# Attention weights times values as three split products, in a hybrid encoder layer on one core

## The reference

```python
def diff_attention(q, k, v, lam, lambda_init, subln_g, rel_table):
    ...
        logits = jnp.einsum('bqhcd,bkhcd->bhcqk', qblk, k,
                            preferred_element_type=F32) * scale + bias[None, :, None]
        p = jax.nn.softmax(logits, axis=-1)
        attn = p[:, :, 0] - lam * p[:, :, 1]
        return jnp.einsum('bhqk,bkhe->bqhe', attn.astype(v.dtype), v)
    ...
    out = rmsnorm(out, subln_g) * (1.0 - lambda_init)
```

## Time and profile before

| | |
|---|---|
| median of 3 runs | 969.24 us (969.03 to 969.33) |
| profiled execution | 969.0 us, its span 967.2 us |
| TensorE busy | 960.2 us, 5755 matmuls |
| VectorE busy | 664.1 us |
| ScalarE busy | 440.0 us |
| GpSimd busy | 88.1 us |

### The profile page before, as it was taken

The page is one execution under the profiler, slowest core; times in us unless marked ns, Lnnn a source line. Parts: engine busy times, 40 slices in busy tenths (PEclk is TensorE's granted clock), DMA queues, the critical chain, the costliest instruction groups (busy, mean ns, idle before and its releaser), DMA issues.

```text
span 967.2 us, 15550 instructions
## 1 busy us (share of the span) xinstructions
PE 960.2 (99%) x5755; PEld 839.7 (87%) x5755; DVE 664.1 (69%) x999; ACT 440.0 (45%) x699; POOL 88.1 (9%) x104
## 2 busy tenths in 40 slices
PE   9999999999999999999999999999999999999998
PEld 7889999999888887677777878889999999988887
DVE  6887886777754438868898755788787677743333
ACT  6445665546333233234454563446565554622222
POOL 0011121210011010000000000011111121000100
PEclk9999999999999999999999999999999999999999
DMA  7356777674433346121221332246777767333322
GB/s 233 136 144 171 197 175 192 167 192 139 138 98 100 98 127 238 66 86 48 82 85 44 124 106 91 99 137 159 188 187 182 190 171 183 99 104 99 89 70 87
DMA packets 55031, 128.69 MB, mean 133 GB/s; under 512 B 5955, under 2 KB 14288, under 8 KB 54725
## 3 DMA queue, kind: packets, MB, share of 16 engines
q1 hardware_dynamic: 44452, 107.31, 34.2%
q0 software_dynamic: 10384, 20.67, 12.3%
q10 hardware_dynamic: 144, 0.05, 0.1%
HBM read 123.78 MB, written 4.22 MB: 132 GB/s over the span
## 4 chain that ended last, share of the span: by engine, by line
PE 94%; DVE 3%; issue 1%; ACT 1%; DMA 0%; DVEq 0%; SPq 0%; ACTq 0%
PE bank L2151 14%; PE bank L2153 14%; PE bank L2152 14%; PE bank L2198 12%; PE bank L2199 12%; PE bank L2200 12%; PE bank L2639 1%; PE bank L2640 1%; PE bank L2641 1%; PE bank L2531 1%; PE bank L2285 1%; PE bank L2286 1%; PE bank L2287 1%; ACT prob L960 0%; PE bank L2365 0%
## 5 line engine op out<-in xcount | busy, mean ns | idle before, releaser
L1216 DVE TENSOR_TENSOR w_lo<-raw,w_hi 128x1024 fp32r<-128x1024 f32 (+1 forms) x94 | 113.3, 1205 | 110.2 <-ACT w_hi L630 109.9
L630 ACT CAST w_hi<-raw 128x1024 fp32r<-128x1024 f32 (+1 forms) x94 | 95.0, 1011 | 187.5 <-PE bank L2153 172.4
L2198 PE MATMUL bank<-xt_hi,w_hi 128*128 128x256 f32 x544 | 154.2, 284 | 0.0
L2199 PE MATMUL bank<-xt_lo,w_hi 128*128 128x256 f32 x544 | 153.9, 283 | 0.0
L2200 PE MATMUL bank<-xt_hi,w_lo 128*128 128x256 f32 x544 | 153.9, 283 | 0.0
L2151 PE MATMUL bank<-x_hi,w_hi 128*128 128x512 f32 x320 | 128.5, 402 | 0.1
L2152 PE MATMUL bank<-h_lo,w_hi 128*128 128x512 f32 x330 | 128.4, 389 | 0.0
L2153 PE MATMUL bank<-x_hi,w_lo 128*128 128x512 f32 x320 | 124.8, 390 | 0.0
L2152 PE MATMUL bank<-x_lo,w_hi 128*128 128x512 f32 x320 | 124.7, 390 | 0.0
L2199 PE MATMUL bank<-xt_lo,wt_hi 128*128 128x256 f32 x408 | 115.5, 283 | 0.0
L2200 PE MATMUL bank<-xt_hi,wt_lo 128*128 128x256 f32 x408 | 115.5, 283 | 0.0
(11 more groups left out here) (370 smaller groups left out, 1856.5 us busy)
## 6 DMA issues: line engine op xcount, KB each, us to landing
raw<-in_ffn_w_down SPq DMA_DIRECT2D x32, 512.0 KB, 3.5
raw<-in_ffn_w_gate SPq DMA_DIRECT2D x25, 512.0 KB, 4.4
raw<-in_ffn_w_up SPq DMA_DIRECT2D x25, 512.0 KB, 4.5
raw<-in_w_in SPq DMA_DIRECT2D x24, 512.0 KB, 3.3
raw<-in_ffn_w_gate SPq DMA_DIRECT2D x34, 256.0 KB, 3.2
raw<-in_ffn_w_up SPq DMA_DIRECT2D x34, 256.0 KB, 3.1
raw<-in_ffn_w_down SPq DMA_DIRECT2D x16, 384.0 KB, 3.1
sums<-in_ffn_w_gate SPq DMA_DIRECT2D x17, 256.0 KB, 3.9
```

The source lines that it names most:

```text
L630: nc.scalar.copy(w_hi[:, half, 0:kb, :], raw[:, slot, 0:kb, :]).then_inc(w_hi_made, 1)
L1216: nc.vector.tensor_tensor(w_lo[:, half, 0:kb, :], raw[:, slot, 0:kb, :], w_hi[:, half, 0:kb, :].bitcast(F32), ALU.subtract).then_inc(w_spl ...
L2198: nc.tensor.matmul(dst, high[:, k, :], xt_hi[ffn][:, m, k, :], start=start and k == 0, stop=False, skip_group_check=True)
L2199: nc.tensor.matmul(dst, high[:, k, :], xt_lo[ffn][:, m, k, :], start=False, stop=False, skip_group_check=True)
```

## The change

The product of weights and values is made as three split products. ScalarE's copies of the turned weights and values now cast to fp32r (`attn_hi`, `v_hi`), and VectorE makes the low parts (`attn_low`, `v_low`), each as the difference of the bank and the high part. The low parts lie where the folded values of the Hyena part (`vx`) and the bias were, for head 3 also in a part of `x0c`. A turn now waits until VectorE has read its bank too (`attn_split` in place of `attn_t_set`). ScalarE's cast of projection weights for one tile per head moves behind the last copies. Two semaphores are taken out and two added (`v_split`, `attn_split`): the landing of the lambdas is counted with another load, and one wait in the filters is made with the chain semaphore of VectorE.

```diff
-        v_nat, _ = place("v_nat", [P, NT, P], at=act3_at)
+        v_hi, _ = place("v_hi", [P, NT, P], F32R, at=act3_at)
+        v_lows = [place(f"v_lo{n}", [P, NT, P], F32R, at=at)[0] for n, at in enumerate((vx_at + 4 * S, bias_at))]
+        attn_hi, _ = place("attn_hi", [P, NT, S], F32R, at=attn_t_at)
+        attn_lows = [place(f"attn_lo{n}", [P, S], F32R, at=at)[0]
+                     for n, at in enumerate((vx_at + 4 * 2 * S, vx_at + 4 * 3 * S, x0c_at + 4 * 3 * S))]
+
+        def v_low_part(h):
+            return v_lows[h == 3]
+
+        def attn_low_part(h, kt):
+            return attn_lows[1 if kt % 2 else 2 * (h == 3)]
...
-                act.wait_ge(mlp_landed, 16)
+                act.wait_ge(mlp_landed, 32)
...
-                nc.scalar.copy(v_nat[:], bank[TURN_BANKS[h]][:].rearrange("p (t c) -> p t c", t=NT)).then_inc(v_set, 1)
+                nc.scalar.copy(v_hi[:], bank[TURN_BANKS[h]][:].rearrange("p (t c) -> p t c", t=NT)).then_inc(v_set, 1)
...
-                    nc.scalar.copy(attn_t[:, kt, :], bank[4 + kt % 2][:]).then_inc(attn_t_set, 1)
+                    nc.scalar.copy(attn_hi[:, kt, :], bank[4 + kt % 2][:]).then_inc(attn_t_set, 1)
...
             attn_turns(0, (0, 1))
-            split(8, N_MIX + 15)
             qk_high(1, 1)
             attn_turns(0, (2, 3))
+            split(8, N_MIX + 15)
             attended(0)
...
-                    nc.vector.tensor_tensor(hsum[:, 0, :], total, decay[:, 0, :], ALU.mult).then_inc(filt_read, 1)
-                    dve.wait_ge(filt_read, 1)
+                    link(nc.vector.tensor_tensor(hsum[:, 0, :], total, decay[:, 0, :], ALU.mult))
...
+            def v_low(h):
+                dve.wait_ge(v_set, h + 1)
+                nc.vector.tensor_tensor(v_low_part(h)[:], bank[TURN_BANKS[h]][:].rearrange("p (t c) -> p t c", t=NT),
+                                        v_hi[:].bitcast(F32), ALU.subtract).then_inc(v_split, 1)
+
+            def attn_low(h, kt):
+
+                dve.wait_ge(attn_turned, NT * h + kt + 1)
+                dve.wait_ge(attn_t_set, NT * h + kt + 1)
+                nc.vector.tensor_tensor(attn_low_part(h, kt)[:], bank[4 + kt % 2][:], attn_hi[:, kt, :].bitcast(F32),
+                                        ALU.subtract).then_inc(attn_split, 1)
...
             combine(0, 3)
+            v_low(0)
             cross_far(0)
             split(8, N_MIX + 14)
+            attn_low(0, 0)
             project(13)
             split_qk(1, 0)
+            attn_low(0, 1)
+            attn_low(0, 2)
             split_qk(1, 1)
+            attn_low(0, 3)
             own_near(0)
             split(8, N_MIX + 15)
...
             hy_low(3)
+            v_low(3)
+            attn_low(3, 0)
+            attn_low(3, 1)
             split(8, N_OUT + 1)
+            attn_low(3, 2)
+            attn_low(3, 3)
             split(8, N_OUT + 2)
...
             def turn(h, kt):
-                wait(pe, attn_t_set, NT * h + kt - 1)
+                wait(pe, attn_split, NT * h + kt - 1)
...
-                pe.wait_ge(v_set, h + 1)
+                pe.wait_ge(v_split, h + 1)
                 for kt in range(NT):
                     pe.wait_ge(attn_t_set, NT * h + kt + 1)
-                    ins = nc.tensor.matmul(bank[6][:], v_nat[:, kt, :], attn_t[:, kt, :], start=kt == 0, stop=kt == NT - 1)
+                    nc.tensor.matmul(bank[6][:], v_hi[:, kt, :], attn_hi[:, kt, :], start=kt == 0, stop=False)
+                    nc.tensor.matmul(bank[6][:], v_low_part(h)[:, kt, :], attn_hi[:, kt, :], start=False, stop=False)
+                    pe.wait_ge(attn_split, NT * h + kt + 1)
+                    ins = nc.tensor.matmul(bank[6][:], v_hi[:, kt, :], attn_low_part(h, kt)[:], start=False, stop=kt == NT - 1)
                     if kt + 2 < NT:
                         turn(h, kt + 2)
```

More of the change, by code:

```diff
@@ L281, in build @@
         x_landed = [sem(f"x_landed{k}") for k in range(KD)]
-        ident_landed, cols_landed, mlp_landed, lam_landed, dft_landed, late_landed, filt_landed = (
-            sem(n) for n in ("ident_landed", "cols_landed", "mlp_landed", "lam_landed",
+        ident_landed, cols_landed, mlp_landed, dft_landed, late_landed, filt_landed = (
+            sem(n) for n in ("ident_landed", "cols_landed", "mlp_landed",
                              "dft_landed", "late_landed", "filt_landed"))
@@ L309, in build @@
             sem(n) for n in ("proj_read", "score_sum", "logit_set", "prob_set", "attn_set", "r0_set"))
-        v_turned, v_set, attn_turned, attn_t_set, pv_sum, att_sq, att_o_set = (
-            sem(n) for n in ("v_turned", "v_set", "attn_turned", "attn_t_set", "pv_sum", "att_sq", "att_o_set"))
+        v_turned, v_set, v_split, attn_turned, attn_t_set, attn_split, pv_sum, att_sq, att_o_set = (
+            sem(n) for n in ("v_turned", "v_set", "v_split", "attn_turned", "attn_t_set", "attn_split", "pv_sum", "att_sq", "att_o_set"))
         tap_set, vx_set, vx_turned, vx_nat_set = (
@@ L423, in others @@
                 sp.dma_start(z_t[:], a["c_z"]).then_inc(mlp_landed, 16)
-                sp.dma_start(lam_in[:].rearrange("p k d -> p (k d)"), a["lambdas"].to_broadcast([P, 4 * DK])).then_inc(lam_landed, 16)
+                sp.dma_start(lam_in[:].rearrange("p k d -> p (k d)"), a["lambdas"].to_broadcast([P, 4 * DK])).then_inc(mlp_landed, 16)
                 sp.dma_start(rel[:], a["rel_bias"]).then_inc(late_landed, 16)
@@ L1096, in _ @@
             attn_turns(1, (0, 1))
-            split(8, N_MIX + 19)
             qk_high(2, 1)
             attn_turns(1, (2, 3))
+            split(8, N_MIX + 19)
             attended(1)
@@ L1112, in _ @@
             attn_turns(2, (0, 1))
-            split(8, N_MIX + 23)
             qk_high(3, 1)
             attn_turns(2, (2, 3))
+            split(8, N_MIX + 23)
             attended(2)
@@ L2004, in _ @@
             imaginary_parities(0)
+            v_low(1)
             project(16)
@@ L2007, in _ @@
             cross_near(1)
+            attn_low(1, 0)
             project(17)
             split_qk(2, 0)
+            attn_low(1, 1)
+            attn_low(1, 2)
             split_qk(2, 1)
+            attn_low(1, 3)
             cross_far(1)
@@ L2032, in _ @@
             real_parities(1)
+            v_low(2)
             project(20)
@@ L2035, in _ @@
             imaginary_parities(1)
+            attn_low(2, 0)
             project(21)
             split_qk(3, 0)
+            attn_low(2, 1)
+            attn_low(2, 2)
             split_qk(3, 1)
+            attn_low(2, 3)
             split(8, N_MIX + 23)
@@ L2431, in two_scores @@
                     pe.wait_ge(logit_set, 2 * NT * h)
-                    pe.wait_ge(attn_t_set, NT * h)
+                    wait(pe, attn_split, NT * h)
                 for q in (qb, qb + 1):
@@ L2485, in turn_v @@
                 pe.wait_ge(spec_read, 2)
-                wait(pe, v_set, h)
+                wait(pe, v_split, h)
                 if h == 3:
@@ L2541, in att_sums @@
                 else:
-                    pe.wait_ge(v_set, 3)
+                    pe.wait_ge(v_split, 3)
                 if h == 2:
@@ L2625, in out_half @@
                     elif pair == 2:
-                        pe.wait_ge(attn_t_set, NT * HEADS)
+                        pe.wait_ge(attn_split, NT * HEADS)
                     elif pair == 3:
```

4 lines of the change are left out of this document (2 added, 2 removed).

## The result

The kernel after takes 974.57 us, the median of 4 runs (974.33 to 974.80); the kernel before, beside it on the same chip, takes 969.13 us (968.87 to 969.33, 4 runs). The ratio is 1.0057 with a 95% interval of 1.0045 to 1.0070: slower by 5.4 us. The forecast was 974.5. The profiled execution of after is 974.8 us with a span of 973.0, 5.8 more than the span of before.

A forecast was written before the change was run, and what follows sets the result against it. TensorE's queue, busy 99%, was taken to bound the kernel, so waits for VectorE's subtractions are lost. Heads 0 to 3 sum 1.3 + 2.2 + 2.2 - 0.1 = +5.6 us on 969.0: 974.6, given as 974.5, range 971.2 to 977.6.

The forecast's parts named there:

- TensorE's own work is less: Weights-times-values block without waits: 3.9 us against 4.49 measured in head 0, 0.6 less, 2.4 over four heads.
- bound of 2.4: The most the change can bring, with every subtraction hidden: -2.4 us, to 966.6.
- One subtraction costs 0.61 of VectorE's queue: On VectorE, each of 20 added subtractions takes 0.61 us of queue, 12.2 us in all.
- The waits in each block: Block changes with TensorE waiting for low parts: head 0 +1.3 us, heads 1 and 2 +2.2 each, head 3 -0.1.
- The signs: Profile after: waits 1.5 to 2, 0.5, 0.3 us; blocks 5.8, 6.9, 6.9, 4.2; VectorE busy +14; wrong if waits below 3.
- rival 2: All heads do as head 3, or the first wait in the block shrinks: 968.6 to 971 us; 10%.
- The head start of the turns: The first two turns of a block come six matmuls ahead; cited in support of rival 2.
- VectorE catches up: VectorE, 0.7 us behind after head 0, clears its backlog in 1.80 us idle before the reciprocal; late logits cost nothing.
- The subtractions hide: In the blocks, VectorE's subtractions cost nothing and TensorE keeps its saving of 2.4 us: 966.6 us; 5%.
- Break-even: Same as rival 2: four blocks at -0.1 to +0.5 us each, 968.6 to 971 us; 10%.
- The backlog is not drained: Late logits delay exponentials, combined weights and the next head's turns, up to 1.5 us in heads 1 and 2: 977.5; 11%.
- The clock falls: Repeated short gaps drop TensorE to 1.2 GHz in the blocks of heads 0 to 2, +11 us: 985; 2%.

The follow-up runs named there:

- Experiment 1: Kernel after without low parts or subtractions; TensorE does three high products per pair and waits only for ScalarE's copies: 967.14 us, ratio 0.9982.
- experiment 4: Kernel after with all four subtractions of heads 0 to 2 ahead of weight split and spectrum products, copies ahead of ScalarE's casts: 970.13 us, ratio 1.0012.
- experiment 3: Kernel after with only the first subtraction of heads 1 and 2 moved ahead of weight split and spectrum products, its copy ahead of `q_hi`: 976.95 us, ratio 1.0082.
- experiment 5: As experiment 4, with VectorE's spectrum steps and weight splits spread over more gaps, parities behind the first logits of head 3: 970.77 us, ratio 1.0019.
- 9: As experiment 5, plus products inside the tile, tile 23's split behind head 3's second logits, first output-projection split behind the last long-convolution gate: 968.50 us, ratio 0.9996.
- experiment 7: As experiment 3, with ten matmuls of 512 columns into an unread bank added in the long wait of heads 1 and 2: 975.79 us, ratio 1.0070.

## Why the prediction was right

**TensorE's own work is less.** Right in kind. Experiment 1 shows it alone: 4.01 us for head 0's block against 3.9 from the rows, and -1.7 us in all. The prediction's bound of 2.4 was too wide, because it had no wait for ScalarE's copy in it: 0.43 in head 1 and the like in head 2. In head 0 two small misses offset: a turn between split products takes 0.36 (462.96 to 463.32 in experiment 1) and not 0.44, and the last product waits 0.16 for its copy.

**One subtraction costs 0.61 of VectorE's queue.** Right: `v_lo` at 493.98 and `q_t` behind it at 494.59 are 0.61 apart. All 16 of `attn_lo` last 0.68 to 0.69 us, though they read PSUM. The busy time rose by 676.0 - 664.1 = 11.9 us, where I had written 20 x 0.69 = 14. That was a slip: overlapping records aren't counted twice on the page, and 20 x 0.61 = 12.2 from the paragraph above it was the number to use.

**The waits in each block.** Right to 0.1 us in each of the four, as the table shows. Within heads 1 and 2 one thing is divided otherwise: I let TensorE wait from 494.90 for the first low part, in one piece. In the trace the first high product already waits 0.34 for ScalarE's copy, behind a `q_hi` that VectorE delivered late, and the third product then waits the rest. The sum is the same, as VectorE's place in the queue sets both ends.

**The signs.** Besides the busy time, one came otherwise than written. The first third product of heads 1 and 2 was to be idle by 1.5 to 2 us; the rows list 1.13 and 1.12, and by starts it is 1.53 - 0.23 = 1.30, with the rest of the 1.9 in front of the first product. For that reason the blocks measured from the first product are 6.46 and 6.47 us and not 6.9 in these two heads; 5.81 and 4.24 in heads 0 and 3 are as written (5.8 and 4.2). The second wait (0.56 by starts in head 1, where 0.5 was written) and the last (0.23 for 0.3) came, and the listed waits for subtractions sum to 4.0, above the 3 below which the prediction called itself wrong.

**Luck in the total.** The mechanism is as forecast, but the agreement to 0.1 us is closer than the working allows, with some 0.1 us of error in each of ten waits; and 0.29 of the span's 5.8 us lies ahead of the blocks, where the prediction had nothing.

**The head start of the turns.** The description ahead of the prediction, and rival 2, say that turns 0 and 1 come before the last two steps, six matmuls, of a tile. The rows show one step, three matmuls (495.28 to 496.21 in head 1 of after). No term of the sum rested on this; it would have given rival 2 less support than I allowed it.

**VectorE catches up.** Right: no wait at the turns or the scores appeared in the waits view of after, and the distances between the blocks are those of before. Turns of head 1 to turns of head 2, less the block, are 34.54 - 8.52 = 26.02 after and 32.34 - 6.34 = 26.00 before.

**The rivals.** *The subtractions hide*: they don't, but experiment 4 shows that most of their cost is a matter of place in the queue. *Break-even*: head 3 alone does it. *The backlog is not drained*: no sign. *The clock falls*: not in this kernel, as the granted clock of the four blocks is 1.00:

```profile
462.50:468.50 6.00, 4.99 (x24) 2.80 (x22) 5.57 (x9) 2.95 (x5) 0.00 (x0) 1.00 0.25 87
494.50:503.00 8.50, 6.58 (x32) 4.00 (x30) 8.04 (x13) 4.23 (x7) 0.00 (x0) 1.00 0.19 64
529.00:537.50 8.50, 6.61 (x32) 4.02 (x30) 7.86 (x13) 4.23 (x7) 0.00 (x0) 1.00 0.00 1
573.30:577.80 4.50, 4.42 (x23) 3.09 (x22) 2.83 (x4) 1.17 (x2) 0.00 (x0) 1.00 0.38 117
```

But the mechanism is real: in experiment 3 one wait of 2.85 us brought it on. The page that the prediction names for it in the Trainium skill ("TensorE: Matmul & The Clock Gate", A second HAM failure mode) speaks of short gaps between groups of matmuls; the repeated short gaps of this block, listed at up to 1.13 us, did not do it.

## What to carry to other kernels

When a step that one engine did alone is handed to a chain of three, the price is read from where the new instruction stands in the helper's queue, and not from how much the helper idles over the span: VectorE was idle 31% of the time, and TensorE waited for it all the same. Count also what the added work pushes back, since 2.9 us of the cost came through instructions that the change had not touched. And before moving one such wait away, look at the next one: moved alone it made the kernel slower, moved together they came due in other tiles, and in experiments 5 and 9 a weight split moved out of the way stood next in front of another result that TensorE waited for.

## What the runs showed of the hardware

- In experiment 3 a single wait of 2.85 us (as the row lists it; 3.25 from start to start) in a kernel that was otherwise busy brought TensorE's clock from 2.4 to 1.2 GHz (granted 0.50) for some 3 us, in head 1 from just before TensorE started again and in head 2 only about 1 us after that. Over two such waits this cost 1.3 us more than the waits. Listed waits of 0.3 to 1.1 us in the blocks of after, and one of 1.30 in experiment 5, left it at 1.00.
- Ten matmuls into a bank that nobody reads, put into each of the two waits (experiment 7), kept it at 1.00 and made the kernel 1.3 us faster.
- At half clock (experiment 3), matmuls of 512 columns stood 0.42 apart and not 0.46, twice 0.23. The granted clock reads 0.50 over the whole of 500.40 to 503.40, so a mixed stretch is not the reason; the distance does not quite double with the clock halved, and the runs don't tell why.
